# Summing the last expert pair into the residual: 0/1 matrix times weighted rows in two rounded parts

## What is computed

```
gates = jnp.sum(jax.nn.one_hot(e_idx, N_EXPERTS) * w_in[..., None], axis=1)   # two non-zero per token
a = jnp.einsum("td,edf->tef", t, w_gate)
u = jnp.einsum("td,edf->tef", t, w_up)
hid = jax.nn.silu(a) * u * gates[:, :, None]
y = jnp.einsum("tef,efd->td", hid, w_down)
x = x + y            # then kv norm (layer 0) or final norm (layer 1)
```

## Time and profile before

| | us |
|---|---|
| median of 3 runs | 1480.1 |
| lowest, highest | 1478.97, 1483.7 |
| the profiled execution, its own time | 1482.62 |
| its span on the core | 1480.8 |
| mean granted TensorE clock | 0.984 of full |

### The profile page before, as it was taken

How to read it: one execution, slowest core, us unless ns; L and a number is a source line. 1 busy time by engine, 2 the same in 40 slices (tenths; PEclk the granted TensorE clock), 3 DMA queues, 4 the chain that set the end, 5 groups by cost and what they waited for, 6 DMA issues and landing times.

```text
span 1480.8 us, 20665 instructions
## 1 busy us (share of the span) xinstructions
PE 1420.7 (96%) x7296; PEld 1156.7 (78%) x7296; DVE 1128.1 (76%) x1647; ACT 785.9 (53%) x1024; POOL 457.8 (31%) x330
## 2 busy tenths in 40 slices
PE   7999997999999997999999999999998899999997
PEld 5889685788888865888888888888887588888863
DVE  6999728888888869766858667585753888888866
ACT  5211835777777736344252533424353677777733
POOL 0000014344444410422405133150402544444310
PEclk9999997999999999999999999999999999999999
DMA  5242516899999954222212122131546599999872
GB/s 218 86 135 90 213 54 258 324 373 380 383 385 393 373 220 179 91 71 71 85 57 99 57 85 71 57 99 57 197 142 239 203 357 378 383 386 376 324 316 107
DMA packets 52765, 309.87 MB, mean 209 GB/s; under 512 B 10544, under 2 KB 16432, under 8 KB 38896
## 3 DMA queue, kind: packets, MB, share of 16 engines
q1 hardware_dynamic: 42128, 291.48, 51.3%
q0 software_dynamic: 9792, 16.80, 3.1%
q10 hardware_dynamic: 800, 1.00, 0.2%
HBM read 299.27 MB, written 28.84 MB: 222 GB/s over the span
## 4 chain that ended last, share of the span: by engine, by line
PE 87%; DVE 6%; DMA 2%; ACT 2%; issue 2%; POOL 0%; SPq 0%; DVEq 0%; POOLq 0%; ACTq 0%
PE PS L2185 5%; PE PS L2186 5%; PE PS L2187 5%; PE PS L2039 4%; PE PS L2038 4%; PE PS L2042 4%; PE PS L2025 4%; PE PS L2026 4%; PE PS L2027 4%; PE PS L2074 3%; PE PS L2075 3%; PE PS L2078 3%; PE PS L2201 3%; PE PS L2203 3%; PE PS L2202 3%; PE PS L2063 2%
## 5 line engine op out<-in xcount | busy, mean ns | idle before, releaser
L832 POOL TENSOR_TENSOR KQ<-rope_ab 64x512 f32<-64x512 f32 x96 | 173.6, 1809 | 316.5 <-DVE rope_ab L1698 312.9
L1573 DVE TENSOR_TENSOR wgl<-WR,wgh 128x2048 fp32r<-128x2048 f32 x66 | 150.9, 2293 | 39.3 <-ACT wgh L999 39.3
L1110 ACT ACTIVATE wh<-wraw 128x1024 fp32r<-128x1024 f32 x76 | 80.3, 1058 | 174.3 <-PE PS L2187 170.0
L1573 DVE TENSOR_TENSOR wul<-WR,wuh 128x2048 fp32r<-128x2048 f32 x66 | 148.4, 2288 | 5.2 <-issue 5.2
L1620 DVE TENSOR_TENSOR wdl<-WR,wdh 128x2048 fp32r<-128x2048 f32 x56 | 128.2, 2289 | 25.8 <-ACT wdh L1032 25.8
L1698 DVE TENSOR_TENSOR rope_ab<-PS,rope_sb 32x512 f32<-32x512 f32 x192 | 131.9, 687 | 2.6
L999 ACT ACTIVATE wuh<-WR 128x2048 fp32r<-128x2048 f32 x66 | 122.8, 1908 | 10.9 <-PE PS L2027 10.9
L1032 ACT ACTIVATE wdh<-WR 128x2048 fp32r<-128x2048 f32 x56 | 107.4, 1919 | 36.6 <-PE PS L2078 36.6
L999 ACT ACTIVATE wgh<-WR 128x2048 fp32r<-128x2048 f32 x66 | 125.1, 1903 | 0.0
L1680 DVE TENSOR_TENSOR wl<-wraw,wh 128x1024 fp32r<-128x1024 f32 x76 | 94.6, 1245 | 31.6 <-ACT wh L1110 30.1
L2038 PE MATMUL PS<-wgh,xgh 128*128 128x512 f32 x264 | 108.7, 412 | 1.4 <-ACT xgh L1015 1.4
(11 more groups left out here) (371 smaller groups left out, 3519.9 us busy)
## 6 DMA issues: line engine op xcount, KB each, us to landing
WR<-w_gate SPq DMA_DIRECT2D x33, 2048.0 KB, 12.0
WR<-w_up SPq DMA_DIRECT2D x33, 2048.0 KB, 9.3
WR<-w_down SPq DMA_DIRECT2D x33, 2048.0 KB, 12.0
wraw<-w_qkv SPq DMA_DIRECT2D x72, 512.0 KB, 3.3
WR<-w_in SPq DMA_DIRECT2D x8, 1024.0 KB, 4.9
xn_dram<-SC SPq DMA_DIRECT2D x8, 512.0 KB, 2.8
SC<-y_dram SPq DMA_DIRECT2D x8, 512.0 KB, 6.0
HT<-y_dram SPq DMA_DIRECT2D x8, 512.0 KB, 9.2
```

The costliest lines, as they stand in the source:

```text
L832: nc.gpsimd.tensor_tensor(to, cos, sin, ALU.add).then_inc(rope_done, 1)
L1573: V.tensor_tensor(lo[:, kts, :], raw[:, kts, :], hi[:, kts, :].bitcast(F32), ALU.subtract).then_inc(done, 1)
```

## The change

The 0/1 matrix takes the place of the weighted one on TensorE, and the weights move to the rows. ScalarE copies both turned matrices out at once and sums each along its tokens as it does (`accum_out`): a slot belongs to one token, so the sum, `slot_w`, is the weight of the slot. VectorE makes of each matrix a 0/1 matrix in the rounded type (`ones_at`). ScalarE scales the down product by `slot_w` into a rounded leading part `yh`; VectorE forms the trailing part `yl`, the product times the weight less `yh`. `sum_rows` now multiplies the 0/1 matrix by `yh` and by `yl`, and accumulates both parts of both blocks in one bank for each half tile: four rounded products per half tile, 32 per layer, whatever `two` is. Six banks are used instead of four, two of them twice. Where there is no second block, GpSimd has zeroed its `yh` and `yl` (`no_second_block`). It does so in either case.

The order changes too. VectorE waits for both copies ahead of the first `add_stored`, and puts the split of block 0 (`trailing_y(0)`) between the third and the fourth. TensorE waits for this split behind down of block 0, makes block 0's products for the first two token tiles, then takes block 1's transposes and down product, and then the rest. The waits on `y_free` go, and so do the separate adds for block 1.

```diff
--- before.py
+++ after.py
@@ -297,7 +297,10 @@
         wdh = at("wdh", 184, [P, FT, 512], F32R)
         wdl = [at(f"wdl{b}", 112 + 16 * b, [P, FT, D], F32R) for b in range(2)]
         hTh = at("hTh", 196, [P, FT, P], F32R)
-        SUM_BANKS = (5, 7, 0, 1)
+        SUM_BANKS = (5, 7, 0, 1, 2, 6, 5, 7)
+        yh = [at(f"yh{b}", 144 + 8 * b, [P, D], F32R) for b in range(2)]
+        yl = [at(f"yl{b}", 148 + 8 * b, [P, D], F32R) for b in range(2)]
+        ones_at = [at(f"ones_at{b}", 160 + 2 * b, [P, T], F32R) for b in range(2)]
 
         o = 0
 
@@ -372,6 +375,7 @@
         last2 = rs(2)
         mix = [rs(2 * NT) for _ in range(2)]
         spread_w = [rs(T) for _ in range(2)]
+        slot_w = rs(2)
         ones48 = cs(MAXC - 1, E)
         limits = cs(MAXC + 1)
         xcols = cs(XB)
@@ -408,7 +412,7 @@
                (0, 1): p_bank[2][:, 0:256], (0, 2): p_bank[2][:, 256:512], (0, 3): p_bank[3][:, :]}]
         sel, pen = (swap_sb[:, P + 8 * k:P + 8 * (k + 1)].rearrange("p (s n) -> p s n", s=2) for k in range(2))
         fin_g = cut(WR, 4096, D)
-        wol_done, presum_done, band_set = [], [], []
+        wol_done, presum_done, band_set, ones_set, y_zeroed = [], [], [], [], []
 
 
         beats = {(l, stage): [] for l in range(2) for stage in ("rank", "rows")}
@@ -477,8 +481,8 @@
         hid_done = [sem(f"hid_done{l}") for l in L2]
         hidT_done = [sem(f"hidT_done{l}") for l in L2]
         y_done = [sem(f"y_done{l}") for l in L2]
-        gh_done, gl_done, uh_done, ul_done, xh_done, xl_done, y_free = (
-            [sem(f"{name}{l}") for l in L2] for name in ("gh_done", "gl_done", "uh_done", "ul_done", "xh_done", "xl_done", "y_free"))
+        gh_done, gl_done, uh_done, ul_done, xh_done, xl_done = (
+            [sem(f"{name}{l}") for l in L2] for name in ("gh_done", "gl_done", "uh_done", "ul_done", "xh_done", "xl_done"))
         y_stored = [[sem(f"y_stored{l}{b}") for b in range(2)] for l in L2]
         att_const, masks_in = sem("att_const"), sem("masks_in")
         wu_raw = [sem(f"wu_raw{s}") for s in range(NU)]
@@ -491,7 +495,7 @@
         fin_in, y_ready, out_stored = sem("fin_in"), sem("y_ready"), sem("out_stored")
 
         sum_mm = [Later(u_mm, KT), Later(conv_mm, len(BY_BANDS))]
-        sum_add = [Later(glu_done, KT), Later(ln_d, KT)]
+        yl_done = [Later(glu_done, KT), Later(ln_d, KT)]
         spread_set = Later(ln_n, KT + 1)
         spread_mm, spread_sb = Later(var_mm, KT), Later(sig_done, KT)
         hTh_done = [Later(wil_done, KT), Later(v_done, 3 * NP_HEADS)]
@@ -714,8 +718,6 @@
         def _(pool):
             steps = Steps(pool, p_steps)
             nc.gpsimd.memset(eps, EPS).then_inc(eps_set, 1)
-            for c, s in enumerate(y_free):
-                nc.gpsimd.memset(spare[:, c:c + 1], 0.0).then_inc(s, 1)
             nc.gpsimd.memset(onesf, 1.0 / D).then_inc(conv_init, 1)
             nc.gpsimd.memset(upad[:, 0:PAD], 0.0).then_inc(conv_init, 1)
             for b in range(2):
@@ -775,6 +777,7 @@
                     gather(b, 0)
                 pool.wait_ge(routed.sem, routed.at(l, 1))
                 last = pool.value_load(last_i[0:1, 0:1], min_val=E // 2 - 1, max_val=(E + XB) // 2 - 1)
+                two = pool.value_load(two_i[0:1, 0:1], min_val=0, max_val=1)
                 before = pool.value_load(last_i[0:1, 1:2], min_val=E // 2 - 2, max_val=(E + XB) // 2 - 2)
 
                 def clear(b):
@@ -786,10 +789,13 @@
                     pool.indirect_dma_start(y_dram[l], bass.IndirectOffsetOnAxis(ap=zcol[b], axis=0), zeros, None,
                                             bounds_check=2 * T - 1, oob_is_err=False).then_inc(y_cleared.sem, 16)
 
-                def stored(n):
-                    for b in range(2):
-                        pool.wait_ge(y_stored[l][b], n * 16)
-                    nc.gpsimd.tensor_tensor(spare[:, 7:8], ident[:, 0:1], ident[:, 0:1], ALU.mult).then_inc(y_free[l], 1)
+                def no_second_block():
+
+                    pool.wait_ge(hid_done[l], 2 * last + two + 2)
+                    nc.gpsimd.tensor_tensor(spare[:, 7:8], ident[:, 0:1], ident[:, 0:1], ALU.mult)
+                    for y in (yh, yl):
+                        steps.mark(nc.gpsimd.memset(y[1][:, :].bitcast(F32), 0.0))
+                    y_zeroed.append(steps.n)
 
                 def pair(i, more):
 
@@ -808,7 +814,7 @@
                 with pool.Fori(1, before) as i:
                     pair(i, True)
                 pair(before, False)
-                stored(last)
+                no_second_block()
 
             moe_pool(0)
 
@@ -1069,11 +1075,13 @@
                 nc.scalar.activation(yst[1][:, 512:1024], PS[4][:, :], ACT.Copy).then_inc(y_done[l], 1)
 
                 def last_pair(i):
-                    def store_y(b):
+                    def weighted_y(b):
+
                         act.wait_ge(down_mm[l], 2 * i + (b + 1))
-                        act.wait_ge(y_free[l], 2)
-                        nc.scalar.activation(yst[0][:, 0:512], PS[3][:, :], ACT.Copy)
-                        nc.scalar.activation(yst[0][:, 512:1024], PS[4][:, :], ACT.Copy).then_inc(y_done[l], 1)
+                        if b == 1:
+                            act.wait_ge(p_steps, y_zeroed[l])
+                        nc.scalar.activation(yh[b][:, 0:512], PS[3][:, :], ACT.Copy, scale=slot_w[:, b:b + 1]).then_inc(hTh_done[l].sem, 1)
+                        nc.scalar.activation(yh[b][:, 512:1024], PS[4][:, :], ACT.Copy, scale=slot_w[:, b:b + 1]).then_inc(y_done[l], 1)
 
                     silu_gate(i, 0)
                     def copy_hidT(b):
@@ -1088,16 +1096,13 @@
                         silu_gate(i, 1)
                     copy_hidT(0)
                     act.wait_ge(spread_mm.sem, spread_mm.at(l + 1))
-                    nc.scalar.activation(spread_w[0], PS[5][:, :], ACT.Copy).then_inc(spread_sb.sem, 1)
-                    store_y(0)
+                    for b in range(2):
+                        nc.scalar.activation(spread_w[b], PS[5 + b][:, :], ACT.Copy, accum_out=slot_w[:, b:b + 1]).then_inc(spread_sb.sem, 1)
+                    act.wait_ge(spread_sb.sem, spread_sb.at(2 * l + 2))
+                    weighted_y(0)
                     with act.If(two > 0):
                         copy_hidT(1)
-                        act.wait_ge(y_done[l], 2 * i + 2)
-                        nc.scalar.activation(yst[1], yst[0], ACT.Copy)
-                        nc.scalar.activation(spread_w[1], PS[5][:, :], ACT.Copy).then_inc(hidT_done[l], 1)
-                        act.wait_ge(hidT_done[l], 2 * i + 3)
-                        nc.scalar.activation(spread_w[0], PS[6][:, :], ACT.Copy)
-                        store_y(1)
+                        weighted_y(1)
 
                 last_pair(last)
 
@@ -1411,17 +1416,12 @@
                 steps.step(V.scalar_tensor_tensor(X[:, n, :], yq[n][0], wt[0][:, n, :], X[:, n, :], ALU.mult, ALU.add))
                 V.scalar_tensor_tensor(X[:, n, :], yq[n][1], wt[1][:, n, :], X[:, n, :], ALU.mult, ALU.add).then_inc(y_added.sem, 1)
 
-            def add_sum(n, h):
-                cols = slice(h * 512, (h + 1) * 512)
-                return V.tensor_tensor(X[:, n, cols], X[:, n, cols], PS[SUM_BANKS[(2 * n + h) % 4]][:, :], ALU.add)
-
-            def add_last(n, l, two):
-
-                if n == 0:
-                    dve.wait_ge(sum_add[l].sem, 2 * NT * two + sum_add[l].at(0))
+            def add_last(n, l):
+
                 for h in range(2):
-                    dve.wait_ge(sum_mm[l].sem, 2 * NT * two + sum_mm[l].at(2 * n + h + 1))
-                    ins = add_sum(n, h)
+                    cols = slice(h * 512, (h + 1) * 512)
+                    dve.wait_ge(sum_mm[l].sem, sum_mm[l].at(2 * n + h + 1))
+                    ins = V.tensor_tensor(X[:, n, cols], X[:, n, cols], PS[SUM_BANKS[2 * n + h]][:, :], ALU.add)
                 ins.then_inc(x_upd.sem, 1)
                 dve.wait_ge(x_upd.sem, x_upd.at(("kv", "out")[l], n + 1))
 
@@ -1659,27 +1659,37 @@
                     with dve.If(two > 0):
                         up_trail(1, 2 * i + 1)
                         hidden(i, 1)
-                    for n in range(NT):
+                    def trailing_y(b):
+
+                        for h, (sem_, n) in enumerate(((hTh_done[l].sem, hTh_done[l].at(2 * i + b)), (y_done[l], 2 * i + (b + 2)))):
+                            dve.wait_ge(sem_, n)
+                            cols = slice(h * 512, (h + 1) * 512)
+                            V.scalar_tensor_tensor(yl[b][:, cols], PS[3 + h][:, :], slot_w[:, b:b + 1], yh[b][:, cols].bitcast(F32),
+                                                   ALU.mult, ALU.subtract).then_inc(yl_done[l].sem, 1)
+
+                    dve.wait_ge(spread_sb.sem, spread_sb.at(2 * l + 2))
+                    for b in range(2):
+                        steps.mark(V.tensor_scalar(ones_at[b][:, :], spread_w[b], 0.0, None, ALU.is_gt))
+                    ones_set.append(steps.n)
```

(52 more changed lines are left out.)

## The result

| | median us | runs |
|---|---|---|
| before | 1481.38 | 6, 1478.97 to 1483.70 |
| changed | 1491.53 | 6, 1489.27 to 1494.88 |
| ratio | 1.0066 | 95% interval 1.0056 to 1.0076 |

The changed kernel is slower by 0.66%, some 10 us, where 6.1 us was forecast and 1490.5 us was the upper end of the range. In the profiled executions the spans differ by 11.7 us: 6.1 in the last pair of layer 0, 4.5 in that of layer 1, 2.3 between the two, less 1.2 ahead of the first.

The account below looks back on a forecast made before the run. TensorE, busy 96% of the span, carried 87% of the chain, though VectorE had no slack in layer 0. +4.3 - 1.0 + 1.4 + 1.4 = +6.1 us on the median 1480.1 gave 1486.2 us, range about 1481.5 to 1490.5.

Parts of the forecast that it names:

- Layer 0's waits: Last pair of layer 0: waits on ScalarE's copies and VectorE's split delay the norm's first reciprocal, +4.3 us.
- Layer 0's clock: Layer 0: TensorE's clock falls behind its longer stand and slows the ten products ahead of the first add, +1.4 us.
- Nothing takes the shift up: Behind layer 0's sums: VectorE and ScalarE work in series in the norm, so the +4.3 us shift stays whole.
- Layer 1, 5.2 us lost and 6.2 gained: Layer 1's last pair: second down product ends 5.2 us later, the way from there to the reciprocal shortens 6.2: -1.0 us.
- At nothing: GpSimd's zeroing: GpSimd's two memsets of 0.95 us end microseconds before TensorE or ScalarE needs them, so they cost nothing.
- Layer 1's clock: Layer 1: low clock behind TensorE's stand slows eight products and the start of the second down product, +1.4 us.
- Rival (b): Both layers: clock stays down longer because sparse work in the tail doesn't raise it, +9.2 us, 1489.3; chance 0.12.
- Rival (c): Both layers: TensorE waits no longer than before, its own work sets the path, -3.4 us, 1476.7; chance 0.07.

Follow-up runs that it names:

- e10: The changed kernel itself, unaltered, measured again beside the other versions: 1494.6 us, ratio 1.0076 to the kernel before.
- e1: Changed kernel with small bf16 products (24 in layer 0, 32 in layer 1) where TensorE waits for block 0's split, every wait kept: 1487.2 us, 1.0038.
- e7: Changed kernel with block 1's 16 products left out in layer 0, where that block is empty: 1491.18 us, 1.0056.
- e11: Changed kernel with the edits of both e3 and e4: 1479.75 us, 0.9981.
- e2: Changed kernel with GpSimd's zeroing put off until block 0's down product is done: 1489.49 us, 1.0045.
- e4: Changed kernel with own banks for the second down product, block 0's products behind it, block 1's hidden rows copied before block 0's weighted rows: 1482.98 us, 1.0001.
- e6: Changed kernel split by case: one block keeps plain fp32 sums; two blocks use e4's banks, stored rows first, matrices and splits beside second down product: 1474.66 us, 0.9945.
- e3: Changed kernel with VectorE's wait for ScalarE's copies and the 0/1 matrices moved behind the three stored tiles: 1486.48 us, 1.0030.
- e8: Kernel before plus one wait: with two blocks, TensorE waits for VectorE's fourth stored tile before turning block 1's hidden rows: 1489.35 us, 1.0043.
- e9: Kernel before with e8's added wait and 24 small bf16 products where TensorE stands for it: 1486.72 us, 1.0028.

## Why the prediction was wrong

The direction and the mechanism of the two waits held; the step was 10.1 us instead of 6.1, because the two terms of the clock were too small and the term of GpSimd's zeroing was put at nothing. Another 1.3 us of the distance to the forecast time is the base: the forecast stood on a median of 1480.1 us for the kernel before, the comparison gave 1481.38. As a step, the upper end of the range was 10.4 us over the kernel before, so the step of 10.1 lies just inside it and the 11.9 of e10 beyond it.

- **Layer 0's waits, +4.3 forecast.** Right. VectorE stood 3.01 us (3.2 forecast), TensorE 4.15 (4.5), and the two 0/1 matrices took 0.76 us (0.9). With the clock kept up (e1) layer 0 is 3.9 us longer than before.
- **Layer 0's clock, +1.4.** Too small: 2.2 us by e1. With it the reciprocal came 6.1 us later against 5.7, relative to `hidden`.
- **"Nothing takes the shift up", and nothing was put behind it either.** From the reciprocal to the first score products of attention it was 55.38 us before and 58.38 in the profiled changed kernel, +3.0: 1.3 with the low clock at the transposes of the norm, the rest with another low stretch in the first products of attention (595.9 to 599.3). Four traces have both of these falls (changed, e7, e10, e11), and in them it is 880.9 to 881.2 us from this reciprocal to the last `hidden` of layer 1, where it was 878.8 before. But e2, whose layer 0 has the same stand of 4.15 us, has neither of the two, only a later one, and 878.1 us. So in an execution that has both they cost some 2.3 us, and that the change brings them is not shown. They are not in the sum below.
- **Layer 1, 5.2 us lost and 6.2 gained, -1.0.** The 6.2 us gain behind the second down product was right: 5.9 us from its end to the reciprocal, as forecast. The loss ahead of it was 10.7 instead of 5.2 plus 1.4 of clock. Two terms failed, the next two.
- **"At nothing: GpSimd's zeroing."** Wrong. The step asked only when its result is needed, not what it runs beside. It held up the 0/1 matrices by 1.8 us and so made the stand longer: 5.38 us, and 3.62 in e2, where 3.8 was forecast.
- **Layer 1's clock, +1.4.** Undersized. It took its length from one low stretch (573.6 to 577). That length did fit the stand it forecast: in e2 the low stretch behind 3.62 us was 3.4 us. But behind 5.38 us of stand the clock stayed low until 1469.7, through 8.7 us of work: products 3.75 us instead of 1.83, transposes 0.85 instead of 0.5, down product 8.82 instead of 7.10, 4.0 in all; 3.8 by e1.
- **Rival (b), the clock stays down longer, 0.12.** In size it was right in both layers, 2.5 and 3.4 us forecast, 2.2 and 3.8 measured. Its reason was not: it laid the length to sparse work in the tail, and the clock was low right behind the stand, through dense products. Its total, 9.2, came near 10.1 in part by luck, since it has no term for the memsets either.
- **Rival (c), TensorE's own work.** Rightly low for this kernel; e4 and e6 show what it would have brought had the split been off TensorE's path.

The sum by the runs: +3.9 (waits, layer 0) +2.2 (its clock) +0.7 (layer 1 with the clock kept up, which is the forecast -1.0 and 1.8 for the matrices against the memsets) +3.8 (clock, layer 1) = +10.6, against +10.1 and +11.9 by the medians. These terms part one trace's difference by e1, so that they add up proves nothing; e2, e3, e4 and e8 with e9 bear them out from outside.

## What to carry to other kernels

Cheaper products are worth nothing where the engine that makes them must first wait for what prepares them: cost a change by the order of the waits, and look for what merely shares a bank with the waiting work. A stand of the matmul engine is to be costed with the clock behind it: in layer 1 that was some 0.7 of the stand's own length again (e8 against e9, and 3.8 us behind 5.38), elsewhere less or nothing (e4's layer 0, e3's). Give each branch of a data-dependent case its own way; the padding that lets both share one was paid in the case that gained nothing.

## What the runs showed of the hardware

- Behind a stand of 4.1 to 5.4 us with dense work on both sides the granted clock was 0.50 in every trace that had one and kept TensorE idle in it (changed, e2, e3, e4, e7, e8, e10). It was low for 6.8 us with the stands of 4.13 to 4.16 us (layer 0 of the changed kernel, e2, e7 and e10; layer 1 of e3 and e8) but for 3.4 us in layer 0 of e4, with the same stand of 4.14 us; it was low for some 10 us with that of 5.38 us (layer 1 of the changed kernel, 1459.5 to 1469.7, of e7 and of e10). In e1, layer 0, with the same wait filled with products, it stayed whole. Stands of about 2 us (layer 0 of e11, 2.31, and of e3, 2.38; attention, 2.0; the last sums of layer 1, 2.2) were followed by it in some traces and not in others. What decides that wasn't tried.
- Small bf16 products on constants held the clock at 1.00 through waits of 4 to 5 us (e1, e9). No price of theirs could be seen: in e9 layer 1 is longer by the 4.2 us of the wait and no more.
- A fp32 to fp32r tensor-scalar of 128x512 takes 0.42 us, and took 2.19 us while GpSimd ran two memsets of 128x1024 (0.95 us each), which were not slowed.
